# Interleaving the two contraction tiles of a weight chunk in the first feed-forward

## The reference, cut to what matters

```
h2 = rms_norm(x, norm2_g)
up = square(relu(h2 @ w_up))        # 1024 x 1024 times 1024 x 4096
x  = x + up @ w_down                # 1024 x 4096 times 4096 x 1024
```

## Time and profile before

| | us |
|---|---|
| median of three runs | 3303.88 |
| the profiled execution | 3300.83 |
| its span | 3299.0 |
| the first feed-forward's matmuls, from about | 559 to 1250 |
| PE busy over the span | 97% |
| DVE, POOL, ACT busy over the span | 63%, 47%, 37% |

### The profile page before, as it was taken

The page is one execution under the profiler, slowest core; times in us unless marked ns, Lnnn a source line. Parts: engine busy times, 40 slices in busy tenths (PEclk is TensorE's granted clock), DMA queues, the critical chain, the costliest instruction groups (busy, mean ns, idle before and its releaser), DMA issues. The chain is left out here.

```text
span 3299.0 us, 42841 instructions
## 1 busy us (share of the span) xinstructions
PE 3197.2 (97%) x15952; PEld 2539.3 (77%) x15952; DVE 2081.1 (63%) x2618; ACT 1225.2 (37%) x2331; POOL 1550.1 (47%) x1644
## 2 busy tenths in 40 slices
PE   8999999999999999999999999989999999999998
PEld 6777887788888877877577788877768778788776
DVE  5544233866666668763856567656034988887888
ACT  4333123422222234323843655453144622322324
POOL 4222334566666643332044156442206267877885
PEclk9999999999999999999999999989999999999998
DMA  3011111111111111121012011134202211111113
GB/s 105 26 27 29 39 36 57 39 52 52 53 53 52 54 45 48 42 57 38 3 51 49 21 32 33 33 109 122 43 23 83 90 48 49 48 58 52 48 48 145
DMA packets 333890, 172.31 MB, mean 52 GB/s; under 512 B 78336, under 2 KB 325632, under 8 KB 333696
## 3 DMA queue, kind: packets, MB, share of 16 engines
q1 hardware_dynamic: 330352, 161.30, 17.3%
q10 hardware_dynamic: 3344, 8.39, 0.7%
HBM read 161.26 MB, written 8.39 MB: 51 GB/s over the span
## 5 line engine op out<-in xcount | busy, mean ns | idle before, releaser
L240 POOL TENSOR_TENSOR ff_lo<-ff_raw,ff_hi 128x256 fp32r<-128x256 f32 x242 | 231.2, 958 | 265.6 <-ACT ff_hi L219 256.3
L471 POOL TENSOR_TENSOR first_lo<-cf_raw,first_hi 128x256 fp32r<-128x256 f32 x242 | 239.6, 1004 | 113.4 <-ACT first_hi L464 112.6
L333 POOL TENSOR_TENSOR om_lo<-out_raw,om_hi 128x256 fp32r<-128x256 f32 x160 | 130.8, 833 | 290.4 <-ACT om_hi L327 289.6
L264 PE MATMUL psum_all<-h_hi,ff_hi 128*128 128x512 f32 x576 | 234.4, 407 | 9.6 <-DVE h_lo L714 3.7
L471 POOL TENSOR_TENSOR ff_lo<-ffp_raw,ff_hi 128x256 fp32r<-128x256 f32 x194 | 169.2, 877 | 143.4 <-ACT ff_hi L464 143.4
L264 PE MATMUL psum_all<-h_hi,ff_lo 128*128 128x512 f32 x576 | 225.6, 392 | 0.0
L264 PE MATMUL psum_all<-h_lo,ff_hi 128*128 128x512 f32 x576 | 225.1, 391 | 0.0
L231 POOL CAST ff_hi<-ff_raw 128x256 fp32r<-128x256 f32 x116 | 57.9, 499 | 316.8 <-PE psum_all L264 301.9
L464 ACT ACTIVATE first_hi<-cf_raw 128x256 fp32r<-128x256 f32 x242 | 100.2, 417 | 269.4 <-PE psum_all L510 250.6
L2653 DVE TENSOR_TENSOR x_resid<-x_resid,psum_all 128x1024 f32<-128x1024 f32 x112 | 136.8, 1221 | 93.7 <-PE psum_all L510 93.1
L240 POOL TENSOR_TENSOR out_lo<-out_raw,out_hi 128x256 fp32r<-128x256 f32 x120 | 116.3, 972 | 164.7 <-ACT out_hi L219 157.7
(11 more groups left out here) (568 smaller groups left out, 9121.8 us busy)
## 6 DMA issues: line engine op xcount, KB each, us to landing
ff_raw<-w_in_dram SPq DMA_DIRECT2D x104, 256.0 KB, 2.9
cf_raw<-ffn_w_up_dram SPq DMA_DIRECT2D x82, 256.0 KB, 2.9
cf_raw<-ffn_w_down_dram SPq DMA_DIRECT2D x52, 256.0 KB, 2.7
ffp_raw<-w_up_dram SPq DMA_DIRECT2D x41, 256.0 KB, 2.7
ffp_raw<-w_down_dram SPq DMA_DIRECT2D x41, 256.0 KB, 2.7
out_raw<-w_out_dram SPq DMA_DIRECT2D x32, 256.0 KB, 2.7
out_raw<-w_in_dram SPq DMA_DIRECT2D x32, 256.0 KB, 2.8
out_raw<-ca_wo_dram SPq DMA_DIRECT2D x32, 256.0 KB, 2.7
```

Source lines behind the costliest of these rows:

```text
L240: self.nc.gpsimd.tensor_tensor(self.lo[slot][:, :], self.raw[raw][:, at:at + 2 * P], self.hi[slot][:, :].bitcast(F32), ALU.subtract).then_ ...
L264: last = self.nc.tensor.matmul(out[:, n:n + step], wt[slot][:, w], x[:, a], start=(k == 0 and m == 0), stop=(k == self.kts - 1 and m == 2))
L333: self.nc.gpsimd.tensor_tensor(self.lo[slot][:, :], self.raw[piece % self.RAWS][:, at], self.hi[slot][:, :].bitcast(F32), ALU.subtract).th ...
L471: self.nc.gpsimd.tensor_tensor(lo, self.source(u, c), hi.bitcast(F32), ALU.subtract).then_inc(self.split_done, 1)
```

## The change

The high and low parts of a chunk get another order of columns. Before, column `n` of tile `k` lay at `k * 128 + n`; now it lies at `2 * n + k`. ACT and POOL walk the tiles in the same order as before and write (POOL also reads the high part) with a step of two elements, and the stationary operand of each matmul is read with a step of two elements, 8 bytes, in place of one. Raw buffers, transfers, sums, activations, PSUM banks, waits and the order of all instructions on all engines stay as they were. The flag `parted` is set for the first feed-forward alone.

```diff
-    def __init__(self, core, sb, units, early=(), of=None, first=0, made=0, place=None):
+    def __init__(self, core, sb, units, early=(), of=None, first=0, made=0, place=None, parted=False):
-        self.core, self.nc, self.units = core, core.nc, units
+        self.core, self.nc, self.units, self.parted = core, core.nc, units, parted
...
-        hi = self.slot(n)[0].rearrange("p (k n) -> p k n", k=2)
-        self.nc.scalar.activation(hi, self.source(u, c), ACT.Copy).then_inc(self.hi_ready, 1)
+        hi, _, source = self.views(u, c)
+        self.nc.scalar.activation(hi, source, ACT.Copy).then_inc(self.hi_ready, 1)
+
+    def views(self, u, c):
+
+        parts = self.slot(self.first[u] + c)
+        if not self.parted:
+            return (*(part.rearrange("p (k n) -> p k n", k=2) for part in parts), self.source(u, c))
+        return (*(part.rearrange("p (n k) -> p k n", k=2) for part in parts), self.source(u, c))
+
+    def block(self, part, k):
+
+        if not self.parted:
+            return part[:, k * P:(k + 1) * P]
+        return part.rearrange("p (n k) -> p k n", k=2)[:, k]
...
-        hi, lo = (part.rearrange("p (k n) -> p k n", k=2) for part in self.slot(n))
+        hi, lo, source = self.views(u, c)
         pool.wait_ge(self.hi_ready, n - self.ahead + 1)
-        self.nc.gpsimd.tensor_tensor(lo, self.source(u, c), hi.bitcast(F32), ALU.subtract).then_inc(self.split_done, 1)
+        self.nc.gpsimd.tensor_tensor(lo, source, hi.bitcast(F32), ALU.subtract).then_inc(self.split_done, 1)
...
-                w = slice(k % 2 * P, (k % 2 + 1) * P)
...
-                        last = self.nc.tensor.matmul(out, wt[:, w], x, start=(start and k == 0 and m == 0),
+                        last = self.nc.tensor.matmul(out, self.block(wt, k % 2), x, start=(start and k == 0 and m == 0),
...
-                                  [kind for kind, _ in self.tiles], of=before, first=before.before)
+                                  [kind for kind, _ in self.tiles], of=before, first=before.before, parted=True)
```

## The result

The changed kernel is slower: 3320.81 us median of five runs (3319.54 to 3321.07) against 3305.15 us of five (3301.74 to 3305.98), a ratio of 1.0049 with a 95% interval of 1.0037 to 1.0060, which is 12 to 20 us. The forecast was 3275 us. The time lies inside the stated range, but on the other side of no change.

The account below looks back on a forecast made before the run. PE was taken as the bound, through the distance between matmul starts times 2892. 3300.83 - 30.7 + 2 = 3272.1 us for the profiled execution; with the median 3.05 above it, the forecast was 3275 us, range 3267 to 3344.

Parts of the forecast that it names:

- The bound and the count: First feed-forward: PE never waits, so time follows the distance between matmul starts, 226.6 ns, times 2892 matmuls.
- the reading of the surplus: PE's fp32r matmuls: 13.3 ns over 512 columns' time come from load and faster stream colliding; equal pace leaves 2.7.
- the term of -30.7 us: First feed-forward's weight loads with a step of 8 bytes: distance falls 10.6 ns to 216.0, times 2892 matmuls.
- the three sets of rows: PE's trace: plain f32 surplus 2.7 ns, none in fp32r at 1.2 GHz, irregular distances when a run starts.
- slower by more collisions: First feed-forward: load costs the stream by memory swept; distance 239.9 ns, 38.5 us more, 3342 us; chance 0.22.
- no change: First feed-forward: surplus is a fixed cost of an fp32r matmul at full clock; time 3304 us; chance 0.23.
- The slower load that sticks out: PE's loads: step halves their pace, next matmul waits, distance grows 71 ns, 206 us more, 3510 us; chance 0.05.
- Plain f32: Rows of 512-column matmuls 429.4 ns apart, 2.7 over two passes, taken as the nearest with load and stream keeping pace.
- The 2 us: First feed-forward's pair units: allowance for small PE waits on POOL's low part, at d near 0.03; ends 0 and 12.
- the prediction's own formula: With each POOL low part longer by d, PE waits 4d - 0.1 us in each of 15 pair units.
- The cover of low part 6: First feed-forward's pair units: POOL finishes it 0.48 us before PE needs it; faster PE leaves about 0.1 us.

Follow-up runs that it names:

- places: Separate program, nothing else running: series of 24 fp32r matmuls varying where loaded and streamed columns begin, load step and column counts; 226.7 ns at step 1, 233.3 at step 2.
- moved256: Kernel before, step 1, with the split buffers of the first phase's weights 256 bytes further in memory; ratio 1.0004.
- moved128: Kernel before, step 1, with the split buffers of the first phase's weights 128 bytes further in memory; ratio 1.0103, 31.5 us slower.
- kinds: Separate program: series of 24 matmuls varying operand type (fp32r, bf16, plain f32), streamed columns and step; 226.7 ns for 512 fp32r columns, 215.8 for bf16.
- write_step: Kernel before, with only ACT and POOL writing (POOL also reading) the first feed-forward's parts with a step of two columns; PE reads neighbouring columns; ratio 1.0003.
- read_step: Kernel before, with only PE's weight loads of the first feed-forward reading with a step of two columns; ratio 1.0052.
- scan: Separate program: series of 40 matmuls, start of loaded columns moved by 16 bytes through 256, at steps 1, 2 and, coarser, 3; none below 226.7 ns.

## Why the prediction was wrong

**The bound and the count held.** PE's distance times 2892 was the right account: 6.5 ns x 2892 = 18.8 us of an 18.7 us longer span. The later median difference of 15.7 us, with its interval of 12 to 20, is in keeping. That the time fell inside the stated range is luck: the range reached that far only for the sake of the rivals, and the sum of the prediction has no term of this sign.

**The step that failed is the reading of the surplus.** I took the 13.3 ns as collisions between two readers at different pace and concluded that a load sweeping 1024 bytes would keep step with the stream, so that 10.6 ns would go. It predicted 216.0 ns; the chip gave 233.1, so the term of -30.7 us came out as +18.8. The pace itself was as assumed: loads of 32, 64, 96 and 128 columns take 108, 134, 161 and 188 ns in `places`, 0.83 ns a column, which is 1.2 GHz, and 64 and 128 at step 2 take 136 and 193. So the load did come to sweep about as fast as the stream, and the surplus did not go.

Runs that leave the pace out refute the reading itself, not its size: a load with step 0, which sweeps nothing, stands at 231.7 ns, one of 32 columns at 230.8, and neighbouring columns from 128 bytes at 232.2 in the kernel. The pace is the same at 0, 128 and 256 bytes, the distance is not. And no series of 512 fp32r columns at step 1 or 2, from whatever series it came, settled below 226.7.

What the three sets of rows did show is confirmed: 2.5 ns over the two passes in plain f32, nothing over at 1.2 GHz, and irregular distances at the start of a run. The last of these was the clue, and I used it only as a sign of a collision. Measured is that the distance has several values at which it can stay, that 544 cycles is the lowest found with 512 streamed columns, and that starts, step and the series before decide which one comes. The layout before, with all buffers at multiples of 512 bytes and step 1, comes to 544; step 2 does not. The change left a good state, it did not remove a cost. That these values come from how load and stream meet in the memory is the reading that fits best, above all since moving both operands by the same 64 or 128 bytes gives 226.7 again; no run shows it directly.

**The rival "slower by more collisions"** had the sign and the place, at 22%. Its mechanism (cost by the memory swept, 239.9 ns, 38.5 us) is refuted by the same runs, and its size is twice what came. **The rival "no change"**, a fixed cost, falls with the starts: at 512 streamed columns the cost is not fixed (226.4 and 232.2 ns in `moved256` and `moved128`).

**The Trainium skill's two rules.** That loading the next weights takes nothing from the running matmul (the Trainium skill, "TensorE: Matmul & The Clock Gate", "Step-by-step: what each phase is for") agrees with bf16, 215.8 ns whatever the step, and the 215.8 worked out from its "Back-to-back issue gap" is met to the digit. For fp32r at 2.4 GHz the trace differs: the load's layout moves the distance from 226.7 to 233.3. The measurement decides. The lines of 16 bytes with at least two hits, of the Trainium skill's "SBUF — State Buffer", "Specifications (TRN2)", fit one thing seen here: the load keeps about its pace at step 2, with two hits a line (188 to 193 ns), and loses it at steps 3 and 4 (253 and 310).

**The slower load that sticks out.** At step 2 it is 5 to 8 ns longer and hidden. The premise was wrong as well: a load of 310 ns leaves the distance at 235.0, so the next matmul does not wait for the load's recorded end.

**Plain f32.** The prediction counts its rows as matmuls; they are records, two for each matmul of the program. Its comparison stands, since each record has its own load and its own 429.4 ns, and `kinds` gives 429.2.

**ACT and POOL.** Their cost was taken as zero and as 2 us. No wait of PE for POOL stands in the first feed-forward of the changed kernel, so it is zero within the noise. The 2 us do not follow from the prediction's own formula either: at d = 0.03 it gives 15 x 0.02 = 0.3 us, and 2 us would need d near 0.06. The cover of low part 6 can only have grown, since PE's six matmuls of a chunk now take 1.40 us in place of 1.36. In `write_step`, with PE at full pace and the subtraction at 747 ns, the kernel is as fast as before (1.0003).

**Left open.** Why the stable distances are at 544 and 560 cycles and what part of the memory or of PE makes them; whether fp32r has the 13.3 ns also with no load at all, which no run separated; and why the changed kernel takes turns of 229 and 238 where `read_step`, with the same reads, has 233 nearly throughout. Such turns are not peculiar to the step: `scan` has them for step 1 from 128 bytes.

## What to carry to other kernels

Where matmuls in fp32r run back to back at full clock, the place of the stationary columns is part of the tuning: keep them adjacent, start split buffers and streamed operands at multiples of 256 bytes, as the series and `moved256` did without loss, and measure the distance between starts after any move of buffers, since a pad of 128 bytes alone cost this kernel 1%. An unexplained surplus in a steady rhythm may be the best of several states and not a cost to be removed; before building on a theory of it, run the operation by itself in the new layout, which here would have given 233.3 ns in one run. And when a rhythm is irregular at the start of each run and then settles, ask what it settles into before asking what it costs.

## What the runs showed of the hardware that was not expected

Fewer streamed columns do not always save time: 504 take the 226.7 ns of 512. An fp32r stream with a step of two takes twice as long (452 ns), while a load with a step of two is itself only 5 to 8 ns longer. A load of 32 fp32r columns takes 108 ns and one of 128 takes 188, so 80 ns of it do not depend on the columns. A start of the split buffers at 128 bytes in place of 0 cost 5.6 ns for every matmul of the first feed-forward (232.2 against 226.6). The distance of a steady series can depend on the series before it (226.7 or 233.4 ns for the same operands). ACT's copy of 256 columns takes 439 ns with a step of 8 bytes on its output against 418, POOL's subtraction 748 against 740.
